# A hybrid decoder layer: the last residual addition of each row tile goes from VectorE to GpSimd

## Chip, cores and metric

The kernel runs on one core of a Trainium2 chip. The metric is the device time of one execution in microseconds (us), lower is better. The kernel before was run three times: 3462.21, 3464.15 and 3467.51 us, median 3464.15 us.

## What is computed

One decoder layer on a sequence of 2048 tokens of width 1024, all float32. A mixer sub-layer (sparse attention with a top-256 indexer, beside a gated linear recurrence) is followed by a gated feed-forward sub-layer; both are normalised on the way in and on the way out. The change lies in the very last line of the second sub-layer:

```python
x  = x + rms_norm(mix, norm_post_mix[l])          # x1 in this text
h2 = rms_norm(x, norm_pre_ffn[l])
ff = jax.nn.silu(jnp.einsum('btd,df->btf', h2, w_gate[l])) * jnp.einsum('btd,df->btf', h2, w_up[l])
ff = jnp.einsum('btf,fd->btd', ff, w_down[l])
x  = x + rms_norm(ff, norm_post_ffn[l])           # the line of the change
```

`rms_norm(ff, gain)` is `ff * rstd * gain`, with one `rstd` for each row, so the line is one scaling and one addition over every row.

## The kernel before, in words

The first phase (to about 925 us) projects the input and runs the recurrence. The second phase, `mixer_phase`, runs attention over 16 blocks of 128 queries and, threaded between its steps, the dense work: output projection, norms and feed-forward. The dense work goes in four slabs s = 0 to 3 of 512 tokens, each of four row tiles i = 0 to 3 of 128 tokens. It is one hand-written list, `items`, and every engine walks the same list in the same order: its `step(n)` does what this engine has to do at item n. `fills` says behind which attention step which items come. The items of slab 3 behind its output projection run at the end of the kernel, without attention beside them (TAIL).

A slab ends with four items `("down", s, NG-1, 1, i)`, one for each row tile. Call their numbers L0 to L3; they are consecutive. The next slab begins with `("out", s+1, 0, 0, i)` at L3+1 and on. For each row tile the end of a slab runs as follows:

- VectorE adds the last TensorE piece into `acc[:, i, :]` (`add_piece`, line 1812).
- ScalarE squares and sums the row (`square`, line 1534), in step Li+2.
- GpSimd turns the sum into `rstd` (`root`, lines 1432 and 1433), in step Li+2.
- VectorE scales (line 1822, called by `finish`) and adds the x1 row (line 1846), in step Li+4. The x1 row was read back from memory into `tile` by SyncE (`load_back`, line 1298).
- SyncE stores the row (`store_out`, line 1308) once `out_ready` says so.
- ScalarE then copies the first piece of the next slab into the same place in `acc` (`evict`, line 1553). It first waits for `out_stored[i]`, the landing of that store. This holds for slabs 1 and 2, whose output pieces ScalarE evicts. Slab 3 gathers in another buffer, `acc_last`, and its pieces are added by VectorE.

At L3+2 ScalarE's step first evicts the piece of L3+1 (row tile 0 of the next slab), and then squares row tile 3 of the ending slab:

```python
if y[0] in ("part", "out", "down") and read_by(y) == "act":
    evict(y)
...
if last_down(n - 2):
    ...
    square(root_no(s, "ff", i), i)
```

`load_back(s, 3)` reuses the place of row tile 0's x1 row and is issued behind `store_out(s, 0)`. Behind `store_out(s, 3)` SyncE issues two loads of gains (`load_gain`, `load_gain_ffn`) and then the first weights of the next feed-forward (`load_unit`, line 1251), which ScalarE and VectorE split into a high and a low part (lines 1529 and 1773).

In the attention between: TensorE computes scores (1938, 1939), VectorE adds the mask (1758), ScalarE takes the exponential (1512), TensorE transposes (1965), ScalarE copies the transposed block (1524), TensorE multiplies by the values (1977).

Of the kernel before, what the change touches and what calls it, by code (L numbers as in the profile page):

```python
# [21 lines left out]
ALU = mybir.AluOpType  # L22
# [34 lines left out]
TS = SB // P  # L57
# [45 lines left out]
def turned_rows(g, eng, link, kept, rt, b):  # L103

    eng.wait_ge(kept.row_in[b % 2], 16 * (b // 2 + 1))
    r = kept.row[:, b % 2, :]
    for c0, n_heads in ((Q0, HEADS + KV), (QI0, IH + 1)):
        x = r[:, c0:c0 + n_heads * HD].rearrange("p (h d) -> p h d", d=HD)
        x1, x2 = x[:, :, 0:ROPE], x[:, :, ROPE:2 * ROPE]
        cos = kept.rope[:, b, 0:1, :].broadcast_to([P, n_heads, ROPE])  # L110
        sin = kept.rope[:, b, 1:2, :].broadcast_to([P, n_heads, ROPE])
        for n, (xx, cs) in enumerate(((x1, cos), (x2, sin), (x2, cos), (x1, sin))):
            last = g.tensor_tensor(rt[:, n, 0:n_heads, :], xx, cs, ALU.mult)
        link(last)
        g.tensor_tensor(x1, rt[:, 0, 0:n_heads, :], rt[:, 1, 0:n_heads, :], ALU.subtract)
        link(g.tensor_tensor(x2, rt[:, 2, 0:n_heads, :], rt[:, 3, 0:n_heads, :], ALU.add))
# [705 lines left out]
def mixer_phase(nc, a, proj_d, mix_d, x1_d, out, kept):  # L822
# [153 lines left out]
    with ExitStack() as ctx:  # L976
# [3 lines left out]
        def sb_two(name, shape, raw_name, raw_shape):  # L980

            at = -(-nc.sbuf_base // 32) * 32
            rounded = sb(name, shape, F32R)
            return rounded, nc.alloc_sbuf_tensor_at(raw_name, raw_shape, F32, offset=at)
# [4 lines left out]
        def sem(name):  # L989
            return ctx.enter_context(nc.semaphore("m_" + name))  # L990
# [40 lines left out]
        hid, tile = sb_two("hid", [P, HID, 2, SB], "tile", [P, HID, D])  # L1031
# [38 lines left out]
        back_in = [sem(f"back_in{n}") for n in range(TS)]  # L1070
# [2 lines left out]
        ss_ready, rstd_ready = sem("ss_ready"), sem("rstd_ready")  # L1073
        x1_ready, xn_ready = sem("x1_ready"), sem("xn_ready")
        h_hi_ready, h_lo_ready = sem("h_hi_ready"), sem("h_lo_ready")
        out_ready = sem("out_ready")
        x1_stored = [sem(f"x1_stored{n}") for n in range(TS)]
        out_stored = [sem(f"out_stored{n}") for n in range(TS)]

# [57 lines left out]
        for key in use:  # L1137
            who = reader[use[key]]
            if who == "pt":
                _, b, h, p = key  # L1140
                pair_read.append((pt_ready, pt_order[b, h, min(2 * p + 1, NCH(b) - 1)] + 1))
            elif who == "h":
                pair_read.append((h_lo_ready, h_order[key] + 1))
            else:
                counts[who] += 1
                pair_read.append((sa_free_act if who == "act" else sa_free_dve, counts[who]))
# [18 lines left out]
        def wait_piece_read(eng, x):  # L1165
            eng.wait_ge(pj_act if read_by(x) == "act" else pj_dve, read_count[x])

        def acc_of(s):

            return acc if s + 1 < NS else acc_last  # L1170

        def item_at(n):
            return items[n] if 0 <= n < len(items) else ("none",)
# [5 lines left out]
        def last_down(n):  # L1179

            return item_at(n)[0] == "down" and item_at(n)[2:4] == (NG - 1, 1)
# [3 lines left out]
        def linker(eng, step):  # L1185

            count = [0]

            def link(ins):
                count[0] += 1  # L1190
                ins.then_inc(step, 1)
                eng.wait_ge(step, count[0])
            return link
# [6 lines left out]
        X_HOME, BACK_HOME = (E0, E1, L0, L1), (E2, L0, L1, E2)  # L1200
# [20 lines left out]
        def root_no(s, what, i):  # L1221

            return 12 * s + root_order.index((what, i))
# [182 lines left out]
        @block.gpsimd  # L1406
        def _(pool):
            g = nc.gpsimd
            link = linker(pool, pool_step)
            def prep(b):  # L1410

                turned_rows(g, pool, link, kept, kept.rt, b)
                r = row[:, b % 2, :]
                if b >= 4:
                    pool.wait_ge(rel_read, idx_order[b - 2, pairs_of(b - 2) - 1, IH - 1] + 1)
                g.tensor_copy(V[:, b, :], r[:, V0:V0 + KV * HD])
                g.tensor_scalar(wis[:, b % 2, :], r[:, WI0:WI0 + IH], IDX_SCALE, None, ALU.mult)\
                    .then_inc(rows_ready, 1)

            pool.wait_ge(kept.const_in, 2 * 16)  # L1420
            prep(1)
            link(g.memset(mhalf[:], -0.5))
            g.iota(iota8[:], [[1, 8]], base=0, channel_multiplier=0,
                   allow_small_or_imprecise_dtypes=True).then_inc(iota_ready, 1)

            def root(n):
                c = slice(n % 12, n % 12 + 1)
                pool.wait_ge(ss_ready, n + 1)
                if n >= 12:
                    used, i = root_user[n % 12]  # L1430
                    pool.wait_ge(used, TS * (n // 12 - 1) + i + 1)
                link(g.tensor_scalar(var[:, c], ss[:, c], EPS, None, ALU.add))
                g.tensor_tensor(rstd[:, c], var[:, c], mhalf[:, 0:1], ALU.pow).then_inc(rstd_ready, 1)

            def step(n):
                for what, back, ends in (("mix", 2, last_out), ("x1", 4, last_out), ("ff", 2, last_down)):
                    if ends(n - back):
                        s, i = item_at(n - back)[1], item_at(n - back)[4]
                        root(root_no(s, what, i))

            def fill(key):
                for n in range(*fills.get(key, (0, 0))):
                    step(n)

            for b in range(NB):
                if b + 2 < NB:
                    prep(b + 2)
                for c in range(pairs_of(b + 1) if 2 <= b + 1 < NB else 0):
                    for h in range(IH):
                        fill(("i", b, c, h))  # L1450
                fill(("s", b))
                for h in range(HEADS):
                    if h + 1 == HEADS:
                        for k in range(3):
                            fill(("O", b, k))
                    fill(("A", b, h))
                    fill(("B", b, h))
                    if h == HEADS - 2 and 2 <= b + 1 < NB:
                        pool.wait_ge(left_ready, b)
                        g.partition_all_reduce(left_all[:], left[:], P, bass.bass_isa.ReduceOp.max).then_inc(left_max, 1)  # L1460
                    fill(("C", b, h))
            for n in range(TAIL[0], LAST_STEP):
                step(n)
# [164 lines left out]
        def _(dve):  # L1628
            v = nc.vector
            link = linker(dve, dve_step)  # L1630
# [189 lines left out]
            def scaled(n, i, to):  # L1820
                dve.wait_ge(rstd_ready, n + 1)
                return v.scalar_tensor_tensor(to, acc_of(n // 12)[:, i, :], rstd[:, n % 12:n % 12 + 1], gain[:], ALU.mult, ALU.mult)  # L1822
# [17 lines left out]
            def finish(s, i):  # L1840
                wait_piece_read(dve, ("down", s, NG - 1, 1, i))
                dve.wait_ge(g_out_in, 16 * (s + 1))
                to = acc_of(s)[:, i, :]
                link(scaled(root_no(s, "ff", i), i, to))
                dve.wait_ge(back_in[i], 16 * (s + 1))
                v.tensor_tensor(to, to, tile[:, BACK_HOME[i], :], ALU.add).then_inc(out_ready, 1)  # L1846

            def step(n):
                x, y, z = item_at(n), item_at(n - 1), item_at(n - 2)
# [34 lines left out]
            for b in range(NB):  # L1884
# [10 lines left out]
                for h in range(HEADS):  # L1895
# [7 lines left out]
                    g = h // 2  # L1903
# [188 lines left out]
def build(nc, a, out):  # L2092
    proj_d = nc.dram_tensor("proj_d", [T, IN_W], F32, kind="Internal").ap()
    mix_d = nc.dram_tensor("mix_d", [T, D], F32, kind="Internal").ap()
    ctx = ExitStack()
    kept = Carried(nc, ctx)
    project_hgrn_phase(nc, a, proj_d, mix_d, kept)
    x1_d = nc.dram_tensor("x1_d", [T, D], F32, kind="Internal").ap()
    mixer_phase(nc, a, proj_d, mix_d, x1_d, out, kept)
    ctx.close()  # L2100
# [27 lines left out]
```

## Time and profile before

| | |
|---|---|
| median of three runs | 3464.15 us |
| the profiled execution | 3466.06 us |
| its span, first to last instruction | 3464.3 us |
| outside the span | 1.8 us |
| TensorE busy | 3249.0 us (94%) |
| VectorE busy | 2250.7 us (65%) |
| ScalarE busy | 1501.0 us (43%) |
| GpSimd busy | 239.8 us (7%) |

In the profile PE is TensorE, DVE is VectorE, ACT is ScalarE, POOL is GpSimd and SP is SyncE, whose rows (SPq) are DMA issues. In a row of the timeline the first number is the start in us from the span's start, the second the duration in us; then come the engine, the line of the kernel, the operation, out<-in with shapes and the count. A bracket gives the idle time of the engine just before and what ended it.

### The profile page before, as it was taken

How to read it: one execution, taken by the hardware profiler on the slowest of the kernel's cores; microseconds unless marked ns; L12 is line 12 of the kernel's file. 1: busy time of each engine (PE TensorE's matmuls, PEld its weight loads, DVE VectorE, ACT ScalarE, POOL GpSimd, SP SyncE). 2: the span in 40 equal slices, each digit the busy share in tenths (PEclk: the TensorE clock that was granted, in tenths of full speed). 3: DMA queues.
4: the chain of work that ended last, by engine and by line, in shares of the span. 5: the costliest groups of instructions: out<-in, count | busy, mean ns of one | idle time of the engine just before them, and what ended most of it. 6: DMA issues, size and time to landing. Idle time of an engine off the chain costs nothing. (4 is left out here: it accounts for less than half of the span.)

```text
span 3464.3 us, 46669 instructions
## 1 busy us (share of the span) xinstructions
PE 3249.0 (94%) x18176; PEld 2868.0 (83%) x18176; DVE 2250.7 (65%) x3722; ACT 1501.0 (43%) x2477; POOL 239.8 (7%) x399
## 2 busy tenths in 40 slices
PE   8989999999788889999979999997999999979998
PEld 8989999998767678888768888886888888868886
DVE  3456666788655676766778676768776865464444
ACT  3444444554354444444445444445454444333222
POOL 0000010000110110010111000002000000010000
PEclk9999999999899899999989999998999999989999
DMA  5434443343321322222332222124121112242233
GB/s 183 154 104 125 139 143 120 106 134 118 116 71 60 120 82 75 86 83 72 130 122 66 79 70 75 65 90 158 62 73 61 55 61 71 95 168 97 95 100 107
DMA packets 147501, 345.75 MB, mean 100 GB/s; under 512 B 15056, under 2 KB 35920, under 8 KB 145232
## 3 DMA queue, kind: packets, MB, share of 16 engines
q1 hardware_dynamic: 144976, 338.55, 29.2%
q10 hardware_dynamic: 2304, 4.20, 0.3%
q8 instruction: 145, 2.38, 0.3%
q14 instruction: 76, 0.62, 0.1%
HBM read 283.38 MB, written 59.31 MB: 99 GB/s over the span
## 5 line engine op out<-in xcount | busy, mean ns | idle before, releaser
L2017 PE MATMUL PJ_d<-h_hi,wd_hi 128*128 128x512 f32 (+1 forms) x1472 | 574.9, 391 | 14.5 <-DVE h_lo L1778 12.9
L2019 PE MATMUL PJ_d<-h_hi,wd_lo 128*128 128x512 f32 (+1 forms) x1472 | 563.2, 383 | 0.0
L2018 PE MATMUL PJ_d<-h_lo,wd_hi 128*128 128x512 f32 (+1 forms) x1472 | 562.1, 382 | 0.0
L1529 ACT ACTIVATE wd_hi<-wd_raw 128x512 fp32r<-128x512 f32 x568 | 345.7, 628 | 250.2 <-DMA wd_raw<-in_w_gu 157.8
L710 PE MATMUL PJ<-w_hi,h_hi 128*128 128x342 f32 (+1 forms) x1280 | 416.2, 325 | 6.8 <-DVE w_lo L539 6.8
L1524 ACT ACTIVATE pT<-SA 128x512 f32<-128x512 f32 (+3 forms) x320 | 156.6, 532 | 588.3 <-PE SA L1965 588.3
L1773 DVE TENSOR_TENSOR wd_lo<-wd_raw,wd_hi 128x512 fp32r<-128x512 f32 x568 | 381.3, 689 | 45.5 <-ACT wd_hi L1529 42.6
L711 PE MATMUL PJ<-w_lo,h_hi 128*128 128x342 f32 (+1 forms) x1280 | 409.4, 320 | 0.0
L712 PE MATMUL PJ<-w_hi,h_lo 128*128 128x342 f32 (+1 forms) x1280 | 409.2, 320 | 0.0
L1758 DVE CUSTOM_DVE_ANT_0 prob<-SA,bias 128x1024 f32<-128x1024 f32 (+7 forms) x192 | 170.1, 911 | 324.2 <-PE SA L1939 323.6
L2017 PEld LDWEIGHTS PJ_d<-h_hi,wd_hi 128*128 128x128 f32 x1472 | 279.3, 190 | 64.5 <-issue 12.6
L2019 PEld LDWEIGHTS PJ_d<-h_hi,wd_lo 128*128 128x128 f32 x1472 | 279.0, 190 | 54.5
L2018 PEld LDWEIGHTS PJ_d<-h_lo,wd_hi 128*128 128x128 f32 x1472 | 279.7, 190 | 48.6
L1977 PEld LDWEIGHTS SC<-V,pT 128*128 128x128 f32 x2176 | 274.4, 195 | 40.3 <-ACT pT L1524 29.1
L1977 PE MATMUL SC<-V,pT 128*128 128x64 f32 x2176 | 272.3, 275 | 21.4 <-ACT pT L1524 21.4
L2042 PE MATMUL PJ_d<-wd_hi,hid 128*128 128x512 f32 x704 | 280.9, 399 | 1.4 <-DVE hid L1799 1.4
L2044 PE MATMUL PJ_d<-wd_hi,hid 128*128 128x512 f32 x704 | 275.5, 391 | 0.0
L2043 PE MATMUL PJ_d<-wd_lo,hid 128*128 128x512 f32 x704 | 275.2, 391 | 0.0
L420 ACT ACTIVATE stage<-PJ 128x342 f32<-128x342 f32 (+1 forms) x160 | 72.6, 454 | 430.7 <-PE PJ L712 430.7
L710 PEld LDWEIGHTS PJ<-w_hi,h_hi 128*128 128x128 f32 x1280 | 243.1, 190 | 10.2 <-DVE w_lo L539 4.4
L711 PEld LDWEIGHTS PJ<-w_lo,h_hi 128*128 128x128 f32 x1280 | 243.6, 190 | 2.6
L712 PEld LDWEIGHTS PJ<-w_hi,h_lo 128*128 128x128 f32 x1280 | 242.8, 190 | 0.0
(202 smaller groups left out, 5791.2 us busy)
## 6 DMA issues: line engine op xcount, KB each, us to landing
wd_raw<-in_w_gu SPq DMA_DIRECT2D x352, 256.0 KB, 3.0
wd_raw<-in_w_down SPq DMA_DIRECT2D x176, 256.0 KB, 2.6
w_raw<-in_w_in SPq DMA_DIRECT2D x40, 684.0 KB, 4.5
w_raw<-in_w_in SPq DMA_DIRECT2D x40, 676.0 KB, 4.4
row_h<-proj_d SPq DMA_DIRECT2D x16, 1024.0 KB, 6.9
proj_d<-stage SPq DMA_DIRECT2D x40, 342.0 KB, 4.5
proj_d<-stage SPq DMA_DIRECT2D x40, 338.0 KB, 5.3
x_d<-acc SPq DMA_DIRECT2D x24, 512.0 KB, 2.6
```

Source lines behind the costliest of these rows:

```text
L710: t.matmul(out, h_hi[:, k, tok], w_hi[:, u, e], start=(k == 0), stop=False)
L711: t.matmul(out, h_hi[:, k, tok], w_lo[:, u, e], start=False, stop=False)
L712: last = t.matmul(out, h_lo[:, k, tok], w_hi[:, u, e], start=False, stop=(k == KD - 1))
L1529: s_.activation(w_hi[:, u % RING, :], w_raw[:, u % RING, :], ACT.Copy).then_inc(w_hi_ready, 1)
L1773: v.tensor_tensor(w_lo[:, u % RING, :], w_raw[:, u % RING, :], w_hi[:, u % RING, :].bitcast(F32), ALU.subtract).then_inc(w_lo_ready, 1)
L1977: last = t.matmul(SC[:, h * HD:(h + 1) * HD], pT[:, m % 2, (kb % 4) * P:(kb % 4 + 1) * P], V[:, kb, g * HD:(g + 1) * HD], start=(kb == 0), ...
L2017: t.matmul(to[:, tok], w_hi[:, r, w], h_hi[:, c, tok], start=(c == 0 and part != 1), stop=False)
L2018: t.matmul(to[:, tok], w_hi[:, r, w], h_lo[:, c, tok], start=False, stop=False)
L2019: last = t.matmul(to[:, tok], w_lo[:, r, w], h_hi[:, c, tok], start=False, stop=(c == KD - 1 and part != 0))
L2042: t.matmul(to, hi, w_hi[:, r, :], start=(k == parts[0]), stop=False)
L2043: t.matmul(to, hi, w_lo[:, r, :], start=False, stop=False)
L2044: last = t.matmul(to, lo, w_hi[:, r, :], start=False, stop=(k == parts[-1]))
```

## The change

`finish` on VectorE now ends with the scaling and signals a new semaphore, `ff_ready`. A new function of GpSimd, `add_back`, waits for `ff_ready` and for the x1 row, adds, and signals `out_ready`. It is called in GpSimd's step Li+4, behind the roots of that step. Nothing else is changed.

```diff
-        out_ready = sem("out_ready")
+        ff_ready, out_ready = sem("ff_ready"), sem("out_ready")
...
+            def add_back(s, i):
+                pool.wait_ge(ff_ready, TS * s + i + 1)
+                pool.wait_ge(back_in[i], 16 * (s + 1))
+                to = acc_of(s)[:, i, :]
+                g.tensor_tensor(to, to, tile[:, BACK_HOME[i], :], ALU.add).then_inc(out_ready, 1)
+
             def step(n):
                 for what, back, ends in (("mix", 2, last_out), ("x1", 4, last_out), ("ff", 2, last_down)):
                     if ends(n - back):
                         s, i = item_at(n - back)[1], item_at(n - back)[4]
                         root(root_no(s, what, i))
+                if last_down(n - 4):
+                    add_back(item_at(n - 4)[1], item_at(n - 4)[4])
...
             def finish(s, i):
                 wait_piece_read(dve, ("down", s, NG - 1, 1, i))
                 dve.wait_ge(g_out_in, 16 * (s + 1))
-                to = acc_of(s)[:, i, :]
-                link(scaled(root_no(s, "ff", i), i, to))
-                dve.wait_ge(back_in[i], 16 * (s + 1))
-                v.tensor_tensor(to, to, tile[:, BACK_HOME[i], :], ALU.add).then_inc(out_ready, 1)
+                scaled(root_no(s, "ff", i), i, acc_of(s)[:, i, :]).then_inc(ff_ready, 1)
```

## Rows read from the trace of the kernel before

**Rows 1.** The page, part 1: busy us of each engine, share of the span, instructions.
```profile
PE 3249.0 (94%) x18176; PEld 2868.0 (83%) x18176; DVE 2250.7 (65%) x3722; ACT 1501.0 (43%) x2477; POOL 239.8 (7%) x399
```
**Rows 2.** Waits, whole span: total us, times, longest us.
```profile
ACT acc L1553 <- DMA out_y<-acc: 19.9, 6, 5.8
```
**Rows 3.** One line's instructions, line 1846: min/median/max ns, first and last start.
```profile
L1846 DVE TENSOR_TENSOR acc<-acc,tile x12: 1224/1224/1227, 1732.4 to 3049.1; 128x1024 f32<-128x1024 f32 x12
```
**Rows 4.** The stores of line 1308: landing, min/median/max.
```profile
DMA to landing us min/median/max: 2.8/3.2/7.4
```
**Rows 5.** Timeline of GpSimd: small operations, and one beside VectorE's addition of 3038.37.
```profile
948.49 0.35 POOL L115 TENSOR_TENSOR xt<-xt 128x80 f32<-128x80 f32 x1
...
951.60 0.23 POOL L1417 TENSOR_SCALAR wis<-xt 128x8 f32<-128x8 f32 x1
...
3038.41 1.26 POOL L1432 TENSOR_SCALAR var_d<-ss_d 128x1 f32<-128x1 f32 x1 [1.60 <-ACT act_up L1534]
```
**Rows 6.** Timeline, slab 0 to slab 1: VectorE.
```profile
1731.04 1.28 DVE L1822 SCALAR_TENSOR_TENSOR acc<-acc,rstd_d,gain 128x1024 f32<-128x1024 f32 x1
...
1736.40 1.22 DVE L1846 TENSOR_TENSOR acc<-acc,tile 128x1024 f32<-128x1024 f32 x1
...
1747.04 1.23 DVE L1758 CUSTOM_DVE_ANT_0 prob<-SA,bias 128x1024 f32<-128x1024 f32 x1
...
1748.63 1.28 DVE L1822 SCALAR_TENSOR_TENSOR acc<-acc,rstd_d,gain 128x1024 f32<-128x1024 f32 x1
```
**Rows 7.** The same stretch: GpSimd, the roots of row tiles 2 and 3.
```profile
1733.75 0.57 POOL L1433 TENSOR_TENSOR rstd_d<-var_d,mhalf_d 128x1 f32<-128x1 f32 x1
1738.29 0.22 POOL L1432 TENSOR_SCALAR var_d<-ss_d 128x1 f32<-128x1 f32 x1 [3.97 <-ACT act_up L1534]
```
**Rows 8.** The same stretch: ScalarE.
```profile
1736.56 0.60 ACT L1553 ACTIVATE acc<-PJ_d 128x512 f32<-128x512 f32 x1 [3.62 <-DMA out_y<-acc]
1737.06 1.05 ACT L1534 ACTIVATE act_up<-acc 128x1024 bf16<-128x1024 f32 x1
...
1740.73 0.60 ACT L1553 ACTIVATE acc<-PJ_d 128x512 f32<-128x512 f32 x1 [0.52 <-DMA out_y<-acc]
...
1760.10 0.63 ACT L1529 ACTIVATE wd_hi<-wd_raw 128x512 fp32r<-128x512 f32 x1 [3.35 <-DMA wd_raw<-in_w_gu]
```
**Rows 9.** The same stretch: SyncE, the store of row tile 3.
```profile
1751.20 0.34 SPq L1308 DMA_DIRECT2D out_y<-acc  x1
```
**Rows 10.** The same stretch: TensorE, two places where it waited.
```profile
1742.78 0.43 PE L1977 MATMUL SC<-V,pT 128*128 128x64 f32 x2 [0.89 <-ACT pT L1524]
...
1762.19 0.69 PE L1977 MATMUL SC<-V,pT 128*128 128x64 f32 x2 [4.24 <-ACT pT L1524]
```
**Rows 11.** Timeline, slab 1 to slab 2: GpSimd.
```profile
2376.28 1.64 POOL L1433 TENSOR_TENSOR rstd_d<-var_d,mhalf_d 128x1 f32<-128x1 f32 x1
```
**Rows 12.** The same stretch: ScalarE.
```profile
2381.68 0.60 ACT L1553 ACTIVATE acc<-PJ_d 128x512 f32<-128x512 f32 x1 [5.80 <-DMA out_y<-acc]
...
2385.28 0.60 ACT L1553 ACTIVATE acc<-PJ_d 128x512 f32<-128x512 f32 x1
2385.77 1.67 ACT L1512 ACTIVATE prob<-prob,nmx 128x1664 f32<-128x1664 f32 x1
```
**Rows 13.** The same stretch: TensorE, the end of its long wait.
```profile
2421.24 1.97 PE L1984 MATMUL SA<-ident,tile 128*128 128x128 f32 x8 [8.28 <-DVE tile L1837]
```
**Rows 14.** Timeline, slab 2 to slab 3: VectorE, addition of row tile 3.
```profile
3049.13 1.23 DVE L1846 TENSOR_TENSOR acc<-acc,tile 128x1024 f32<-128x1024 f32 x1 [0.43 <-DMA tile<-x_d]
```
**Rows 15.** The same stretch: ScalarE, the first split of the next weights.
```profile
3060.63 0.63 ACT L1529 ACTIVATE wd_hi<-wd_raw 128x512 fp32r<-128x512 f32 x1 [14.61 <-DMA wd_raw<-in_w_gu]
```
**Rows 16.** Timeline, end of the kernel: VectorE and GpSimd.
```profile
3450.68 1.28 DVE L1822 SCALAR_TENSOR_TENSOR acc_last<-acc_last,rstd_d,gain 128x1024 f32<-128x1024 f32 x1
...
3450.99 1.41 POOL L1433 TENSOR_TENSOR rstd_d<-var_d,mhalf_d 128x1 f32<-128x1 f32 x1
...
3459.58 1.23 DVE L1846 TENSOR_TENSOR acc_last<-acc_last,tile 128x1024 f32<-128x1024 f32 x1 [0.25 <-DMA tile<-x_d]
```

## The prediction

> **What bounds the kernel now.** I read the busy times first [rows 1]: TensorE is busy for 94% of the span, VectorE for 65%, GpSimd for 7%. On the averages the change looks free: it takes work from a busier engine and gives it to one with nothing to do. But an average does not say what the moved work is waited for by. All 16 moved additions lie at four places, the ends of the four slabs, so I read these places in the timeline, one engine after the other, and the waits that end there.
>
> At the first two slab ends, ScalarE waits for the store of the very rows that `finish` completes: six waits, 19.9 us in all [rows 2]. The reader should see in the timeline of ScalarE that at 1736.56 and 1740.73 it starts late because of `out_y` [rows 8], and at 2381.68 again, after 5.80 us of waiting [rows 12]. ScalarE is a queue. Behind that wait stand the square of row tile 3, the copies of transposed probabilities and the next exponential, and TensorE waits for those copies [rows 10]. So where the addition now stands, its end already sets the pace, through store, eviction and exponential. A second path leaves from the store of row tile 3: behind it SyncE issues two gains and then the next weights, for which ScalarE waits until 1760.10 [rows 8, 9] and until 3060.63 [rows 15].
>
> **Price of the parts.** *Removed from VectorE:* 16 additions of 1.22 us [rows 3] and a wait of the engine for its own scaling, which costs nothing that can be seen. That is 19.6 us of VectorE. What of it lies on the path is gained, the rest only makes VectorE idle longer.
>
> *Added on GpSimd:* 16 additions of two float32 tensors, 128x1024. The trace has none so long. The nearest rows are an addition of 128x80 in 0.35 us and an operation of 128x8 in 0.23 us [rows 5]. The step between them, 0.12 us for 72 columns, gives 0.35 + 944 x 0.00167 = 1.9 us. If all of the 0.35 us grew with the columns it would be 1024 / 80 x 0.35 = 4.5 us. I take 2.2 us, near the lower end, because most of the 0.35 us is there in the 8-column operation too. The Trainium skill (GPSIMD Engine Reference, Performance versus the Vector engine) gives 4497 ns for an addition of twice this length against 2293 ns on VectorE; half of it, an estimate, is 2.2 to 2.3 us, and the sum would be the same by it.
>
> *Waiting for the other engine.* A 128x1 operation on GpSimd took 1.26 us where VectorE added two SBUF tensors, and one of 128x8 took 0.23 us elsewhere [rows 5]. The same is seen at the end: a root begun at 3450.99 took 1.41 us [rows 16] in place of 0.57 us [rows 7], and ended just behind the scaling of 3450.68 to 3451.96. So an addition on GpSimd that meets a scaling waits up to 1.28 us for it. Whether VectorE is held in turn, no row shows, since GpSimd's operations there are tiny: bounds are nothing, and 2.2 us at each meeting (rival 2).
>
> *The new wait and its queue.* `add_back` makes GpSimd wait for the scaling and for the x1 row. It stands behind the root of its own step. In step L3+1 that is the root of row tile 2, then addition 0; in step L3+2 the root of row tile 3, then addition 1. The root of row tile 3 needs its square. In ScalarE's program this square stands behind the eviction of the next slab's first piece, and this eviction waits for the store of row tile 0. Before, VectorE's `finish` of row tile 1 needed only its own root: its addition ran at 1736.40 [rows 6], before the square of row tile 3 at 1737.06 [rows 8]. After the change the order is forced: addition 0, store, eviction, square 3, root 3, addition 1, store, eviction 1. This is the costly part of the change, and it follows from queue order alone.
>
> **Slab 0 to 1.** The root of row tile 2 takes 0.57 us from 1733.75, but 0.4 us of its start was waiting behind the addition that now goes; it would end near 1733.9 [rows 7]. Addition 0 then ends at 1736.2, or at 1737.4 if it first waits for the scaling of row tile 1; before, it ended at 1733.6 (1731.04 + 1.28 + 0.04 + 1.22, [rows 3, 6]). The landing moves along, so the eviction at 1736.56 goes to 1739.2 to 1740.4. From eviction to the end of root 3 it took 2.6 us (0.5 to the square at 1737.06, 1.2 for square and read-out, 0.9 for the root [rows 7, 8]), so root 3 ends at 1741.8 to 1743.0 and addition 1 at 1744.0 to 1745.2, against 1737.6. Its store lands and the eviction at 1740.73 becomes 1747.1 to 1748.3, 6.4 to 7.6 us late. The exponential and the copy behind it are as late, and so is TensorE at 1742.78 [rows 10]. Two us of scores later VectorE can mask, at 1751.2 to 1752.4 in place of 1747.04; then, 1.6 us on, comes the scaling of row tile 3 [rows 6], its 1.3 us, and addition 3, which ends at 1756.3 to 1757.5. So SyncE stores row tile 3 5.2 to 6.4 us later than 1751.20 [rows 9], the weights come as much later, and TensorE, which waited for them by way of ScalarE for 4.24 us, goes on at 1762.19 plus as much [rows 10]. What TensorE lost at 1742.78 is hidden in that wait. I take 6 us.
>
> **Slab 1 to 2.** The root of row tile 2 ends at 2377.9 (2376.28 + 1.64 [rows 11]), so addition 0 ends at 2380.2 to 2381.0 against 2378.7, and the eviction at 2381.68 is 1.5 to 2.3 us late [rows 12]. Again 2.6 us to root 3, then 2.2 us of addition and 3 us of store (issue and landing, 3.2 us in the median [rows 4]): eviction 1 can run at 2391 to 2392 in place of 2385.28, and the exponential at 2385.77 is 5.7 to 6.6 us late. From there TensorE works without a pause until its wait of 8.28 us, which ends at 2421.24 [rows 13]; the masks and norms that end this wait hang on TensorE's last scores before it, and about 1 us of slack lies between. Here the store of row tile 3 is not late, since its scaling waits for no score. I take 4.5 us, bounds 3 and 6.
>
> **Slab 2 to 3.** There is no eviction by ScalarE, so no ring. Addition 3 waits for its x1 row at 3049.13 [rows 14] and takes 1.0 us more. Additions 1 and 2 come up to 2.5 us later, and the transfers behind them push the weights that ScalarE waits 14.61 us for [rows 15]. I take 2 us, bounds 0.5 and 3.
>
> **The end.** Scaling 0 starts at 3450.68. Before, scaling and addition alternated on VectorE and the last addition ended at 3460.8 [rows 16]. Now GpSimd does addition 0, root 3 (0.9 us) and additions 1 to 3. With no meeting: 3452.4 + 4 x 2.2 + 0.9 = 3462.1, 1.3 us later. If each engine waits for the other: scalings 0 and 1 to 3453.2, addition 0 to 3455.4, root 3 behind scaling 2 to 3457.3, then one scaling more or less hidden and three additions, 3465.3, 4.5 us later. Nothing runs beside this, and the store behind it is the same. Since the rows show GpSimd waiting each time, I take 4 us.
>
> Sum: 6 + 4.5 + 2 + 4 = 16.5 us, bounds 10 and 20. The profiled execution would go from 3466.06 to 3482.6 us. It lies 1.9 us above the median of the three runs, so the median goes from 3464.15 to 3480.7 us.
>
> **Rivals.**
>
> 1. *The delay is absorbed.* ScalarE has idle time of 3 to 6 us at each of these waits, and TensorE has waits of 4.24 and 8.28 us behind them [rows 8, 10, 12, 13]. If these take up the lateness, the end alone stays: 1 to 5 us, 3465 to 3469 us. Against it: TensorE's wait of 4.24 us is itself ended by the late store. Chance 0.15.
>
> 2. *VectorE is held too.* Each addition that starts on GpSimd holds up the next VectorE operation with two SBUF inputs, up to 2.2 us in place of the 1.22 us that VectorE saves: about 1 us more at each of some eight meetings in the busy stretches, so 8 us on top, 3488 us, between 3482 and 3500. For it speaks that the rows show the wait in one direction; against it that many of VectorE's operations there read PSUM. The Trainium skill (SBUF — State Buffer, Who interferes with whom) says that an operation of VectorE with two SBUF inputs and one of GpSimd that reads SBUF hold each other off for the whole instruction, whichever starts first. By that rule the trace agrees in the one direction that it can show. Chance 0.18.
>
> 3. *Faster: VectorE's relief carries through.* Its place is the first two slab ends, where VectorE has little idle time. If root 3 is not late, scaling 3 comes after three additions fewer, 3.7 us earlier, and addition 3 ends 1 us later than on VectorE, so the store at 1751.20 comes 2.7 us earlier, and the same at slab 1: 5.4 us and, with VectorE free for the next norms, up to 12 us gained, less 1 to 3 us at the end. This gives 3452 to 3461, say 3456 us. It decides from the point where addition 1 ends before the eviction of its row tile is due (1740.73). Against it: the queue order above. Chance 0.07.
>
> **Chances.** Forecast 0.60, with its own range 3471 to 3490. I call a change within 0.2% (6.9 us, about what a measurement of this kernel can tell from no change) the same: that is rival 1. Slower takes the forecast and rival 2: 0.78. The range reaches from 3466 (rival 1's greater part) to 3494 (rival 2's greater part); outside are rival 3, a little of rival 1, and the slow end of rival 2.
>
> **What would show it.** Right: on GpSimd, addition 1 stands behind root 3 and both behind the eviction that waits for `out_y`; ScalarE's waits for `out_y` grow from 19.9 us to some 35; additions of 2.0 to 3.5 us; TensorE's wait before 1762 longer or equal but its end 6 us later. Wrong: an addition of 4 us would add some 3 x 1.8 us in the first ring alone, and addition 1 before square 3 would take away the ring. The prediction also fails if TensorE makes up the lateness later, which would show as the same start of the last slab's feed-forward.

## The result: slower by 0.55%, and the profile after

The changed kernel takes 3483.24 us in the median of four runs (3482.59 to 3488.39), the kernel before 3464.63 us beside it (four runs). The ratio is 1.0055, 95% interval 1.004 to 1.007. So the change costs 18.6 us. The profiled execution took 3482.81 us with a span of 3480.9 us, 16.6 us more than the span before.

First the page of the changed kernel, busy times, which answers [rows 1]:

```profile
PE 3254.4 (93%) x18176; PEld 2873.0 (83%) x18176; DVE 2244.3 (64%) x3706; ACT 1500.0 (43%) x2477; POOL 279.7 (8%) x415
```

GpSimd works 40 us more, for 16 instructions more. VectorE has 16 instructions less, but only 6.4 us less work, not 19.6 us. The views of two lines tell why (min/median/max in ns, first and last start in us): line 1439 is the new addition, line 1830 the scaling, which nobody has changed.

```profile
L1439 POOL TENSOR_TENSOR acc<-acc,tile x12: 2337/2472/3296, 1731.3 to 3060.6; 128x1024 f32<-128x1024 f32 x12
...
L1830 DVE SCALAR_TENSOR_TENSOR acc<-acc,rstd_d,gain x24: 1271/1279/2856, 1199.4 to 3058.3; 128x1024 f32<-128x1024 f32 x24
L1830 DVE SCALAR_TENSOR_TENSOR acc_last<-acc_last,rstd_d,gain x8: 1277/1280/3359, 3076.8 to 3469.7; 128x1024 f32<-128x1024 f32 x8
```

An addition on GpSimd takes 2.34 us alone and up to 3.3 us where it meets VectorE. The scaling, with a median of 1.28 us, has cases of 2.86 us, and of 3.36 us at the end of the kernel. In all, the scalings took 40.9 us of VectorE before and 47.2 us after, and the splits of weights (line 1773 before, 1781 after) 381.3 and 385.5 us. These two make up most of the 13.2 us that are missing.

The waits of the whole span (total us, times, longest us), which answer [rows 2]; the prediction had said some 35 us:

```profile
ACT acc L1561 <- DMA out_y<-acc: 36.7, 7, 9.7
```

Here is the timeline of the changed kernel from slab 0 to slab 1, GpSimd, then ScalarE, then VectorE, then TensorE. Its answers of before are [rows 6, 7, 8, 10].

```profile
1730.72 0.57 POOL L1433 TENSOR_TENSOR rstd_d<-var_d,mhalf_d 128x1 f32<-128x1 f32 x1
1731.26 2.39 POOL L1439 TENSOR_TENSOR acc<-acc,tile 128x1024 f32<-128x1024 f32 x1
1738.87 0.61 POOL L1432 TENSOR_SCALAR var_d<-ss_d 128x1 f32<-128x1 f32 x1 [5.23 <-ACT act_up L1542]
1739.56 0.89 POOL L1433 TENSOR_TENSOR rstd_d<-var_d,mhalf_d 128x1 f32<-128x1 f32 x1
1740.43 4.71 POOL L1439 TENSOR_TENSOR acc<-acc,tile 128x1024 f32<-128x1024 f32 x2
...
1737.15 0.60 ACT L1561 ACTIVATE acc<-PJ_d 128x512 f32<-128x512 f32 x1 [6.82 <-DMA out_y<-acc]
1737.65 1.05 ACT L1542 ACTIVATE act_up<-acc 128x1024 bf16<-128x1024 f32 x1
...
1745.86 0.60 ACT L1561 ACTIVATE acc<-PJ_d 128x512 f32<-128x512 f32 x1 [5.06 <-DMA out_y<-acc]
...
1733.58 1.27 DVE L1830 SCALAR_TENSOR_TENSOR acc<-acc,rstd_d,gain 128x1024 f32<-128x1024 f32 x1
...
1750.58 1.23 DVE L1766 CUSTOM_DVE_ANT_0 prob<-SA,bias 128x1024 f32<-128x1024 f32 x1 [7.21 <-PE SA L1944]
...
1752.17 1.28 DVE L1830 SCALAR_TENSOR_TENSOR acc<-acc,rstd_d,gain 128x1024 f32<-128x1024 f32 x1
...
1740.36 3.02 PE L1982 MATMUL SC<-V,pT 128*128 128x64 f32 x16 [3.78 <-ACT pT L1532]
...
1747.90 0.69 PE L1982 MATMUL SC<-V,pT 128*128 128x64 f32 x2 [4.30 <-ACT pT L1532]
...
1766.98 0.69 PE L1982 MATMUL SC<-V,pT 128*128 128x64 f32 x2 [4.32 <-ACT pT L1532]
```

The ring of the prediction is there, step by step: addition 0 (1731.26), its store, the eviction that waited 6.82 us for it, square 3 (1737.65), root 3 (1738.87), and only now additions 1 and 2 (1740.43), then the store of row tile 1 and the second eviction (1745.86). TensorE waits 3.78 us for a copy behind the first eviction and 4.30 us for one behind the second, where before the second wait was 0.89 us. Its later wait is nearly as long as before, 4.32 for 4.24 us; it only comes later. The four scalings of this slab end take 1.27 to 1.28 us each (two are shown), so none is held up here.

To see where the whole difference arises, I compare the start of the same instruction in two kernels, the exponential of the same attention step (line 1512 before, 1520 after), and at the far end the activation of the same feed-forward piece. The "lateness" of a kernel at a time is its start minus that of the kernel before. The table gives how much the lateness grows in each stretch of the profiled executions, times being those of the kernel before. What precedes the first slab end in a profiled execution (-2.6 us in the changed kernel, -2.7 to +3.8 us in the others) is no work of the change and is left out. Each row is one profiled execution. The row of e6, an edit that brings nothing in the medians, shows that a stretch can move by up to 1 us by itself (+0.8 and -1.0, which cancel).

| kernel | slab end 1, 1730 to 1900 | slab end 2, to 2433 | 2433 to 2448 | to 3017 | slab end 3, to 3433 | end |
|---|---|---|---|---|---|---|
| changed | +7.3 | +1.7 | +2.4 | +1.5 | +2.1 | +4.2 |
| e1 | -0.2 | +1.7 | +2.4 | +1.6 | +4.2 | +5.2 |
| e2 | +3.4 | +1.3 | +2.6 | -0.1 | +0.4 | +4.4 |
| e3 | -0.2 | 0 | 0 | 0 | +0.2 | +4.2 |
| e4 | +6.6 | +1.5 | +2.4 | +1.6 | +0.5 | -0.2 |
| e5 | +3.5 | -1.6 | +2.3 | +1.7 | +1.0 | -0.7 |
| e8 | -0.2 | -2.2 | +2.5 | +1.8 | +1.0 | -0.7 |
| e6 | +0.1 | 0 | 0 | +0.8 | -1.0 | +0.3 |
| e7 | -9.7 | -2.3 | +2.8 | +0.2 | +2.5 | -0.7 |
| e9 | -9.6 | -2.4 | +2.9 | +0.1 | -0.2 | -0.9 |
| e10 | -8.7 | -3.5 | 0 | +0.3 | +0.6 | +4.2 |
| e11 | -8.7 | -3.6 | 0 | 0 | +0.8 | -1.3 |

The first row adds up to 19.2 us; less 2.6 us this is the 16.6 us of the spans. Two stretches need a look of their own. At the second slab end, this is the changed kernel on ScalarE, TensorE and SyncE (SPq), which answers [rows 12, 13]:

```profile
2388.47 0.60 ACT L1561 ACTIVATE acc<-PJ_d 128x512 f32<-128x512 f32 x1 [8.02 <-DMA out_y<-acc]
...
2397.04 1.67 ACT L1520 ACTIVATE prob<-prob,nmx 128x1664 f32<-128x1664 f32 x1
...
2410.24 1.67 ACT L1520 ACTIVATE prob<-prob,nmx 128x1664 f32<-128x1664 f32 x1
...
2391.68 3.67 PE L1982 MATMUL SC<-V,pT 128*128 128x64 f32 x16 [4.01 <-ACT pT L1532]
2427.57 1.97 PE L1989 MATMUL SA<-ident,tile 128*128 128x128 f32 x8 [7.18 <-DVE tile L1845]
...
2400.80 0.34 SPq L1308 DMA_DIRECT2D out_y<-acc  x1
```

The same places in the kernel before, beside [rows 12, 13]: the next exponential, TensorE's short wait and the store of row tile 3.

```profile
2404.45 1.67 ACT L1512 ACTIVATE prob<-prob,nmx 128x1664 f32<-128x1664 f32 x1
...
2384.89 3.47 PE L1977 MATMUL SC<-V,pT 128*128 128x64 f32 x16 [1.79 <-ACT pT L1524]
...
2394.76 0.34 SPq L1308 DMA_DIRECT2D out_y<-acc  x1
```

The kernel came here 4.6 us late. The exponential at 2397.04 is 11.3 us later than in [rows 12], so the ring makes it 6.7 us late. But the next exponential (2410.24 after, 2404.45 before) is only 5.8 us later, so 1.2 us is left of it. TensorE had other work queued: in all of this it has one wait, of 4.01 us (1.79 us before), until the wait of 7.18 us that was 8.28 us before. The wait of 4.01 us ends with a copy that stands behind the first eviction, not the second. That eviction is 2.2 us late by the longer addition 0 (3.06 us), and as much in e1 below, which has no ring.

The second look: TensorE's busy time and granted clock (the column PEclk, as a share of full speed) in stretches of 4 us behind this slab end, before and after.

```profile
2432.00:2436.00 4.00, 3.06 (x15) 3.10 (x15) 3.89 (x7) 3.21 (x6) 0.00 (x0) 0.62 0.30 112
2436.00:2440.00 4.00, 4.00 (x36) 4.00 (x36) 2.16 (x4) 1.43 (x3) 0.00 (x0) 0.96 0.01 4
2440.00:2444.00 4.00, 4.00 (x31) 3.74 (x30) 2.87 (x3) 2.13 (x3) 0.00 (x0) 1.00 0.00 0
```

```profile
2436.00:2440.00 4.00, 0.74 (x3) 0.77 (x4) 3.64 (x6) 4.00 (x8) 1.18 (x2) 0.50 0.72 259
2440.00:2444.00 4.00, 4.00 (x22) 4.00 (x20) 3.89 (x6) 1.53 (x2) 0.00 (x0) 0.50 0.01 3
2444.00:2448.00 4.00, 4.00 (x22) 4.00 (x23) 0.53 (x2) 0.77 (x2) 0.00 (x0) 0.54 0.02 4
2448.00:2452.00 4.00, 4.00 (x32) 3.74 (x30) 2.14 (x3) 2.79 (x3) 0.00 (x0) 1.00 0.00 0
```

In both kernels TensorE works in short bursts between waits before this, and its clock falls to the lower level, 1.2 GHz (0.50; the stretch from 2432 has 0.62 before). Before, the clock is back at 0.96 in the first 4 us in which TensorE is busy throughout. After, TensorE works through 8 us at 0.50 and 0.54. These 2.4 us are lost by the clock, not by a wait: TensorE's wait just before this work is 3.77 us in both traces.

### The profile page after: what moved, and what is told of

The parts are those of the page before. It is cut to its first block and busy times, and to the rows that moved or that the text cites. A ratio compares the mean times of both kernels' runs of the same rounds, so it can differ in the third digit from the quotient of the medians.

```text
span 3480.9 us, 46669 instructions
## 1 busy us (share of the span) xinstructions
PE 3254.4 (93%) x18176; PEld 2873.0 (83%) x18176; DVE 2244.3 (64%) x3706; ACT 1500.0 (43%) x2477; POOL 279.7 (8%) x415
## 3 DMA queue, kind: packets, MB, share of 16 engines
q8 instruction: 145, 2.38, 0.3%
## 5 line engine op out<-in xcount | busy, mean ns | idle before, releaser
L1781 DVE TENSOR_TENSOR wd_lo<-wd_raw,wd_hi 128x512 fp32r<-128x512 f32 x568 | 385.5, 697 | 50.2 <-ACT wd_hi L1537 47.2
```

Source lines behind the costliest of these rows:

```text
L1781: v.tensor_tensor(w_lo[:, u % RING, :], w_raw[:, u % RING, :], w_hi[:, u % RING, :].bitcast(F32), ALU.subtract).then_inc(w_lo_ready, 1)
```

## The experiments

My theory at the start had three parts. The loss at the first two slab ends comes from the order in the queues (addition 1 behind root 3, root 3 behind the eviction that waits for store 0). The loss at the end comes from the longer additions themselves. And the holding of VectorE by GpSimd is real but cheap. The rival was that this holding (rival 2 of the prediction) costs the time.

### The ring taken away: e1 and e2

e1 calls the addition ahead of the roots in GpSimd's step, so that addition 1 does not wait for root 3:

```diff
             def step(n):
+                if last_down(n - 4):
+                    add_back(item_at(n - 4)[1], item_at(n - 4)[4])
                 for what, back, ends in (...):
                     ...
-                if last_down(n - 4):
-                    add_back(item_at(n - 4)[1], item_at(n - 4)[4])
```

> The changed kernel, but in each step of GpSimd the addition stands ahead of the roots, so addition 1 no longer waits for root 3 (and with it for square 3, eviction 0 and the landing of store 0). Ring theory: at the first slab end the addition of row tile 1 begins before the square of row tile 3, ScalarE's second wait for out_y there shrinks from 5.06 us to under 2 us, the lateness of 7.4 us falls to 1 to 3 us and that of 4.2 us at the second slab end to 1 to 2 us. The median falls from 3483 to about 3474 us (3471 to 3477). Rival, that the length of the additions and the shared port make the time: nothing of that is changed, so 3481 to 3485 us.

Measured: 3478.88 us (3475.48 to 3483.61), ratio 1.0038 (1.0023 to 1.0052). GpSimd's timeline in e1, slab 0 to slab 1, and ScalarE's second eviction:

```profile
1734.91 2.40 POOL L1439 TENSOR_TENSOR acc<-acc,tile 128x1024 f32<-128x1024 f32 x1 [3.23 <-DVE acc L1830]
...
1739.22 2.41 POOL L1439 TENSOR_TENSOR acc<-acc,tile 128x1024 f32<-128x1024 f32 x1
1742.07 1.22 POOL L1432 TENSOR_SCALAR var_d<-ss_d 128x1 f32<-128x1 f32 x1 [0.44 <-ACT act_up L1542]
...
1744.63 0.60 ACT L1561 ACTIVATE acc<-PJ_d 128x512 f32<-128x512 f32 x1 [0.64 <-DMA out_y<-acc]
```

Addition 1 now comes before root 3, the second eviction waits 0.64 us in place of 5.06, and the loss at slab end 1 goes from 7.3 us to nothing. The additions are as long as before and meet VectorE as often. So at slab end 1 this order carries the whole loss. At slab end 2 nothing changes (+1.7 and +2.4 us), though the ring is gone there too: the ring was no part of what is lost there. The time is above the 3471 to 3477 us that I expected, for two reasons. The second slab end did not fall to 1 to 2 us. And slab end 3 costs 4.2 us in place of 2.1, and the end 5.2 in place of 4.2. There roots now stand behind additions, and at the end VectorE waits 3.28 us for one.

e2 takes the ring away from the other side. ScalarE's step squares row tile 3 before the eviction:

```diff
                 x, y = item_at(n), item_at(n - 1)
+                if last_down(n - 2):
+                    ...
+                    square(root_no(s, "ff", i), i)
                 if y[0] in ("part", "out", "down") and read_by(y) == "act":
                     evict(y)
```

> The changed kernel, but ScalarE squares the row tiles of the ending slab ahead of the eviction in the same step. The queue order on GpSimd stays (root 3 ahead of addition 1), but root 3 no longer hangs on store 0. Ring theory: root 3 of the first slab end starts within 1 us of its place in the kernel before (relative to the scaling of row tile 0), and the median is 3474 to 3477 us. Rival, that GpSimd's queue order alone (an addition that stands behind any root) costs the time: 3481 to 3485 us.

Measured: 3477.84 us (3476.52 to 3480.75), ratio 1.0037 (1.0023 to 1.0051). Slab end 1 costs 3.4 us, half of before: root 3 now stands between additions 0 and 1 with no wait, but its two operations take 1.8 us there, and the first eviction still waits 6.49 us. So half of the loss is the dependence on the eviction; the other half stays as long as the root stands between the additions. The time is just above the expected 3474 to 3477 us.

The same edit in the kernel before the change is e6, a control: does the order of ScalarE alone bring anything?

> The kernel before, with ScalarE's squares of the ending slab ahead of the eviction in the same step. In the kernel before root 3 is not needed until the scaling of row tile 3, some 10 us later, so by the ring theory nothing changes: within 3 us of the kernel before. Rival, that square 3 behind the eviction already costs time there: 3 us or more faster.

Measured: 3466.32 us, ratio 1.0003 (0.9994 to 1.0012). It brings nothing. What e2 gains it gains from the ring.

### The slab ends apart: e3 and e4

e3 leaves the additions of slabs 0 to 2 on VectorE and moves only those of the last slab; e4 moves only those of slabs 0 and 1:

```diff
-                if last_down(n - 4):
+                if last_down(n - 4) and item_at(n - 4)[1] == LAST:      # e3
+                if last_down(n - 4) and item_at(n - 4)[1] < 2:          # e4
                     add_back(item_at(n - 4)[1], item_at(n - 4)[4])
```

> Only slab 3 adds on GpSimd, the other twelve additions are VectorE's as in the kernel before. The steps of my sum stand alone if they add up: 4.2 us over the kernel before, 3468.8 us (3467 to 3471), and the stretch up to the last matmul as before. Rival, that the time lost at the end is a consequence of lateness earlier: within 1.5 us of the kernel before.

Measured: 3469.82 us (3467.33 to 3472.26), ratio 1.0016 (1.0006 to 1.0026). The profiled execution shows the change where it is and nowhere else: +4.2 us at the end. These are VectorE and GpSimd at the end of e3:

```profile
3448.96 5.75 DVE L1830 SCALAR_TENSOR_TENSOR acc_last<-acc_last,rstd_d,gain 128x1024 f32<-128x1024 f32 x3
3455.58 3.25 DVE L1830 SCALAR_TENSOR_TENSOR acc_last<-acc_last,rstd_d,gain 128x1024 f32<-128x1024 f32 x1 [0.86 <-POOL rstd_d L1433]
...
3450.64 2.99 POOL L1439 TENSOR_TENSOR acc_last<-acc_last,tile 128x1024 f32<-128x1024 f32 x1
3453.72 1.08 POOL L1432 TENSOR_SCALAR var_d<-ss_d 128x1 f32<-128x1 f32 x1
3454.88 0.57 POOL L1433 TENSOR_TENSOR rstd_d<-var_d,mhalf_d 128x1 f32<-128x1 f32 x1
3455.41 7.91 POOL L1439 TENSOR_TENSOR acc_last<-acc_last,tile 128x1024 f32<-128x1024 f32 x3
```

Three scalings take 5.75 us where three of 1.28 us need 3.8, and the last one takes 3.25 us, beginning with the additions on GpSimd. The engines hold each other. The additions in a row on GpSimd carry the path to the last store.

> Only slabs 0 and 1 add on GpSimd. If the steps add up: 7.4 + 4.2 us over the kernel before, 3476 us (3473 to 3479), with ScalarE's two grown waits for out_y at each of the two slab ends as in the changed kernel. Rival, that TensorE makes the lateness up later: under 3470 us.

Measured: 3478.44 us (3475.13 to 3481.6), ratio 1.0038 (1.0024 to 1.0053). The end costs nothing and slab end 3 only 0.5 us, while slab ends 1 and 2 are as in the changed kernel. In the medians, e3's 5.8 us and e4's 14.4 us make 20.2 us, for 18.6 us in the changed kernel, so the parts add up within 2 us.

### The addition halved, and replaced by a write: e5 and e8

e5 leaves out the x1 row in half of the columns, and e8 leaves out the addition and writes zeros. Both are for measuring only.

```diff
-                g.tensor_tensor(to, to, tile[:, BACK_HOME[i], :], ALU.add).then_inc(out_ready, 1)
+                g.tensor_tensor(to[:, 0:512], to[:, 0:512], tile[:, BACK_HOME[i], 0:512], ALU.add).then_inc(out_ready, 1)   # e5
+                g.memset(to, 0.0).then_inc(out_ready, 1)                                                                  # e8
```

> The changed kernel, but GpSimd adds only the first 512 of the 1024 columns (the residual of the other half is left out). Theory, that each stage's loss is made of lengths of additions in series: the addition falls from 2.4 to about 1.25 us; the first slab end loses 3 to 4.5 us in place of 7.3 (additions 0, 1 and 3 are in series there), the second 1.2 us less, the end of the kernel 0 to 1 us in place of 4.2 (four in series). Median about 3471 us (3468 to 3474). Rival, that the queue order costs the time whatever the length: the ring stays whole, and the median stays above 3478 us.

> The changed kernel, but GpSimd writes zeros over the rows in place of adding (no reading; the result is left out). It asks what holds VectorE up: in the changed kernel a scaling that begins inside an addition of GpSimd takes up to 3.25 us in place of 1.28. If GpSimd's reading of two tensors holds VectorE's second input up, all scalings take 1.28 us here (maximum under 1.4 us). If any long operation of GpSimd does, some still take over 1.6 us. The time would be 3465 to 3472 us if the writing takes about 1 us.

Measured: e5 3470.64 us (3467.89 to 3475.08), ratio 1.0017 (1.0008 to 1.0026); e8 3465.66 us in one run, which has no interval. Here are the addition's line and the scaling's in e5, then the same in e8:

```profile
L1439 POOL TENSOR_TENSOR acc<-acc,tile x12: 1262/1294/1947, 1731.9 to 3053.2; 128x512 f32<-128x512 f32 x12
...
L1830 DVE SCALAR_TENSOR_TENSOR acc<-acc,rstd_d,gain x24: 1272/1278/2096, 1200.9 to 3051.0; 128x1024 f32<-128x1024 f32 x24
```

```profile
L1439 POOL MEMSET acc<- x12: 947/952/958, 1731.2 to 3048.5; 128x1024 f32 x12
...
L1830 DVE SCALAR_TENSOR_TENSOR acc<-acc,rstd_d,gain x24: 1276/1279/1285, 1199.8 to 3046.3; 128x1024 f32<-128x1024 f32 x24
```

GpSimd's time goes with its columns: 1.26 us for 512, 2.34 us for 1024. The longest scaling shrinks with it, and where GpSimd only writes, no scaling is held at all: the longest of 24 takes 1.285 us, for 2.86 us in the changed kernel. The order of the queues is the same in all three. Slab end 1 costs 7.3, 3.5 and -0.2 us, and at slab end 2 e5 and e8 even gain 1.6 and 2.2 us before the clock (I had expected 1.2 us from e5 there). It is the length of the additions inside the ring that costs. In e8 the ring is still there: the second eviction (1742.49) is 4.4 us late against the kernel before, and this is made up by 1800. ScalarE's waits for `out_y` are 27.4 us in sum there, for 19.9 us before, without a loss, so their sum alone is no measure of the loss. The holding and the length shrink together in these two runs. At slab end 1 the trace of the changed kernel tells them apart, since no scaling is held there; for the other slab ends there is e10.

### The store earlier: e7, e9, e10, e11

If late stores are what costs time, then in the kernel before they cost time too: there ScalarE waits 19.9 us for them [rows 2]. e7 is the kernel before with `finish` in VectorE's step Li+3 in place of Li+4:

```diff
-                if last_down(n - 4):
-                    finish(item_at(n - 4)[1], item_at(n - 4)[4])
+                if last_down(n - 3):
+                    finish(item_at(n - 3)[1], item_at(n - 3)[4])
```

> The kernel before, with VectorE's scaling and addition one item earlier (step Li+3 in place of Li+4). If the stores of the finished rows set the pace at the slab ends, as my reading of the kernel before says, then what comes earlier is gained just as what comes later was lost: ScalarE's waits for out_y shrink from 19.9 us to under 10 us, the store of row tile 3 at the first two slab ends leaves some 6 us earlier, and the time falls by 4 to 9 us, to 3455 to 3460 us. Rival, that these waits are cover for something else: within 2 us of the kernel before.

Measured: 3460.42 us (3457.96 to 3462.72), ratio 0.9984 (0.9975 to 0.9993), just above the expected 3455 to 3460 us. Slab end 1 gains 9.7 us, but slab end 3 loses 2.5 us: there VectorE waits 2.08 us for the x1 row at 3043.03, ahead of the split that TensorE needs, and TensorE starts at 3046.20 after 7.01 us of waiting. e9 keeps the old step for slab 2 alone:

> The kernel before, with the finish of each feed-forward half (scaling, addition and store) one step earlier, as in the run that did this for all slabs (3460.42 us against 3465.63), but slab 2 keeps the old step. In that run the end of slab 3's first half cost some 2.7 us, where VectorE waited for a row of x ahead of its other work. Theory: that cost belongs to the moved finish of slab 2, so keeping it there gives it back: 3457 to 3460 us, ratio 0.9977. Rival: the late row comes from the earlier slabs' gain in time, not from slab 2's step: the same as that run, 3460 to 3462 us.

Measured: 3457.40 us (3454.67 to 3461.38), ratio 0.9978 (0.9968 to 0.9988). Slab end 3 is back at -0.2 us, as the theory said, although the intervals of e7 and e9 overlap.

e10 is the sharpest run for the question of this text. It is the changed kernel, with the scaling on VectorE and the addition on GpSimd both a step earlier. All 16 additions are still on GpSimd, and addition 1 no longer stands behind root 3:

```diff
-                if last_down(n - 4):
-                    add_back(item_at(n - 4)[1], item_at(n - 4)[4])
+                if last_down(n - 3):
+                    add_back(item_at(n - 3)[1], item_at(n - 3)[4])
...
-                if last_down(n - 4):
-                    finish(item_at(n - 4)[1], item_at(n - 4)[4])
+                if last_down(n - 3):
+                    finish(item_at(n - 3)[1], item_at(n - 3)[4])
```

> The changed kernel with scaling, addition and store one step earlier, so that addition 1 no longer stands behind root 3 in GpSimd's order and store 3 leaves earlier. Theory: the slab ends lose time only because the stores are late for the evictions, and so do not lose here: 3468 to 3473 us (the end of the kernel still pays 4.2 us), and ScalarE's waits for out_y are under 10 us in sum. Rival: what is lost at the slab ends comes from GpSimd's additions holding VectorE's scalings and masks, which an earlier step does not change: 3478 us or more.

Measured: 3459.06 us (3457.51 to 3461.69), ratio 0.9983 (0.9974 to 0.9992). That is far below my 3468 to 3473 us: I had expected the losses to vanish and had not counted the gain that e7 already showed. The waits of e10 for the store, and the lines of the addition and of the scaling:

```profile
ACT acc L1561 <- DMA out_y<-acc: 2.9, 3, 1.9
```

```profile
L1439 POOL TENSOR_TENSOR acc<-acc,tile x12: 2343/2404/2779, 1727.4 to 3037.1; 128x1024 f32<-128x1024 f32 x12
...
L1830 DVE SCALAR_TENSOR_TENSOR acc<-acc,rstd_d,gain x24: 1270/1279/3324, 1200.3 to 3032.6; 128x1024 f32<-128x1024 f32 x24
```

The additions are as long as in the changed kernel, and scalings are held even longer (3.32 us for 2.86). The two kernels differ only in the step in which scaling and addition are called, and slab ends 1 to 3 (without the clock) go from +11.1 to -11.6 us. In e9, with every addition on VectorE, they give -12.2 us. (In e7, where slab 2 also ends a step earlier, it is -9.5 us.) So length and holding together cost under 1 us in sum at the slab ends, once hardly a store is late for its eviction, and a stretch moves by as much in e6. Only the end keeps its 4.2 us.

e11 is e10 with the four additions of the last slab back on VectorE:

> The changed kernel with scaling, addition and store one step earlier (3459.06 us), and the four additions of the last slab back on VectorE. In the profiled execution of the run without the latter the lateness against the kernel before is -12.0 us at 3433 us and -7.8 at the end, so the end pays 4.2 us. Theory: this comes back whole, since the end of the kernel is a chain on GpSimd and VectorE that no other work covers: 3455 us (3453.5 to 3457), ratio 0.997. Rival: half of it is the ordinary end of the earlier step (the earlier store finds a slower queue), and comes back only in part: 3457 us or more.

Measured: 3453.47 us (3452.64 to 3455.83), ratio 0.9964 (0.995 to 0.9977), the fastest of all these kernels. In its profiled execution the end gives -1.3 us in place of +4.2, so the end's price comes back whole. Against e9 the interval does not tell whether GpSimd's 12 additions are worth anything: 0.995 to 0.9977 and 0.9968 to 0.9988 overlap. In the profiled executions e11 is 2.7 us ahead of e9 by the sums of the table, and e9 alone has the +2.9 us of the clock from 2433 to 2448.

## Why the prediction was right, and where it was not

The forecast was 3480.7 us in a range of 3466 to 3494, slower with 0.78. It came to 3483.24. The mechanism that carried the largest term is shown. That the sum came so close is in part luck: the second term came out by another mechanism, and things not forecast add to it and take from it.

**The addition.** I took 2.2 us between 1.9 and 4.5. It takes 2.34 us alone and 2.47 us in the median of the busy stretches. Counting from two small rows gave the right order. The Trainium skill (GPSIMD Engine Reference, Performance versus the Vector engine) has 4497 ns for twice the length. Half of it, an estimate, is 2.25 us, and the trace agrees within 4%.

**Slab end 1: 6 forecast, 7.3 measured.** The order was as worked out. I put eviction 1 at 6.4 to 7.6 us late; with the 2.6 us added that the execution was ahead it was at 1748.5, 7.7 us late (1740.73 in [rows 8]). The rest of the term was too small behind it. From the end of TensorE's wait (1747.90) to the mask (1750.58) it is 2.7 us, for the "two us of scores" of the prediction, with the clock at 0.50; then addition 3 takes 2.41 us for 2.2. So the store of row tile 3 was 7.4 us late, for 5.2 to 6.4. TensorE's slow stretch behind its wait of 3.78 us, 3.02 us in place of 2.00, lies ahead of a longer wait and costs nothing. e1, e10 and e8 confirm by three different edits that order and length together make this loss.

**Slab end 2: 4.5 forecast, 4.1 measured, but for another reason.** Here a step failed: "from there TensorE works without a pause", by which the late exponential should have moved everything behind it. The exponential was 6.7 us late, as forecast (5.7 to 6.6), but TensorE had other work queued and 5.5 us of this disappeared. That was rival 1, absorption, and it is right at this place: e1 has no ring and loses the same. A second step also failed: "here the store of row tile 3 is not late". It was issued at 2400.80 for 2394.76, that is 1.4 us late beyond the 4.6 us with which the kernel arrived, most of it the longer addition 3 (2.38 for 1.23 us). The weights came 1.2 us late behind it, and 1.7 us of lateness was left at 2433. e1, without a ring, has the same store 1.4 us late and the same 1.7 us. With the earlier step (e10) this place gains 3.5 us. The rest, 2.4 us, is the late return of the clock, which I had not thought of. That 4.1 us came near the forecast of 4.5 is luck.

**Slab end 3: 2 forecast, 2.1 measured.** ScalarE waited 16.85 us for the weights at 3074.04, for 14.61 in [rows 15]. e4, with VectorE's additions here, has 0.5. The term is no fixed price of the additions: it is 0.4 us in e2, whose additions there are as long and in the same order, and 4.2 in e1, where roots wait behind additions. So the 2 us fit in number; what makes them in one kernel and not in the other is not shown.

**The end: 4 forecast, 4.2 measured.** In the changed kernel, e3 and e10 it is 4.2 each time, and gone in e4 and e11. This is the chain of the changed kernel near its end, in order of time:

```profile
3463.41 1.04 POOL rstd_d L1433
3464.45 0.34 issue
3464.79 2.99 POOL acc_last L1439
3467.86 1.08 POOL var_d L1432
3469.10 0.46 issue
3469.56 2.96 POOL acc_last L1439 x2
```

**Not forecast.** Between 2448 and 3017 the changed kernel loses 1.5 us more, by a dip of the granted clock to 0.65 at 2892 to 2896 (1.00 before). And its execution was 2.6 us ahead before the first slab end, where nothing was changed. One adds, the other takes away. Without both, 17.7 us stand against the 16.5 us of my sum, and 2.4 of the 17.7 are clock. The medians differ by 18.6 us, the profiled executions by 16.75, so some 2 us are the spread between executions.

**Rival 2, holding in both directions.** I gave it 0.18 and 8 us. Its mechanism is real and shown: scalings of up to 3.36 us, a pair of splits of 3.45 us at 2390.66, and none held beside a write. Its price is what I had too high: under 1 us in slab ends 1 to 3 (e10 against e9). That VectorE does nothing there that TensorE waits for next is how I explain it; no run shows this by itself. At the end it is part of the 4.2 us. The Trainium skill (SBUF — State Buffer, Who interferes with whom) says that a GpSimd operation that reads SBUF and a VectorE operation with two SBUF inputs shut each other out for a whole instruction. By the runs the trace agrees in both directions.

**Rival 3, faster.** It was wrong for this change. e10, the kernel with all additions on GpSimd and the order changed, is faster than before, 0.9983, but this is no proof of the rival: e7, in the same step with all additions on VectorE, has 0.9984. The gain is the earlier step's. No run shows that VectorE's relief is worth anything.

**Left open.** The return of the clock 2.3 to 2.9 us late appears in the changed kernel and e1, e2, e4, e5, e7, e8, e9, but not in e3, e6, e10, e11. e7 and e9 have no addition on GpSimd, so it is not owed to these; what decides it I have not settled. There is one profiled execution of each kernel, so whether it belongs to the kernel or to the execution is open as well. The dip at 2892 (in e1, e4, e5, e8, not in e2) is open too.

## What to carry to other kernels

An idle engine is a place in a queue. Before moving an operation to it, write down what stands before the operation there, and follow each of these back until no wait is left: a ring such as "store, eviction, square, root, addition, store" cannot be seen in any busy time. If the traces show waits for the result already (19.9 us here), first ask whether it can be issued a step earlier; this alone was worth 8 us (e9), and 12 us together with twelve additions on GpSimd (e11), two results whose intervals overlap. At the very end of this kernel nothing covered the slower engine, and its price, 4.2 us, was paid in full.

## What I had not expected of the hardware

GpSimd writing 128x1024 float32 took 0.95 us and held no scaling of VectorE (longest 1.285 us of 32); GpSimd adding two such tensors took 2.34 us and stretched scalings of 1.28 us to as much as 3.36 us. A GpSimd operation on 128x1 took 1.08 to 1.22 us beside a scaling, for 0.22 us alone. And the same matrix work, behind the same wait of 3.77 us, found the granted clock back at full in one kernel and at 0.50 for 8 us in the other, which is 2.4 us, more than the direct loss at that place.
